# Two rearrangements in a hybrid-trunk kernel: the order of the matmuls inside a weight piece, and the addresses of its SBUF tiles

## The chip, the cores and the metric

The kernel runs on one core of one Trainium2 chip. The metric is the device time of one execution in microseconds. The kernel before takes 2270.38 us as the median of 3 runs (2270.03 to 2270.39).

## The reference, cut to what matters

Two layers act on 256 tokens of width 2048. Each has a token mixer (banded attention in the first layer, a gated linear recurrence in the second), a cross attention into 256 memory tokens, an output projection and a SwiGLU feed-forward part. Nearly all arithmetic is in the projections, each of the form "256 x K activations times K x N weights", in float32:

```python
mem_kv = rms_norm(mem, norm_mem[i]) @ w_mem_kv[i]
q_a, k_a, v_a, q_m = _split(h @ w_in_a[j], A_SPLITS)          # even layer
q_b, f_b, i_b, g_b, q_m = _split(h @ w_in_b[j], B_SPLITS)     # odd layer
x = x + jnp.concatenate([mix, mem_out], axis=-1) @ w_o[i]
gate, up = _split(rms_norm(x, norm_ffn[i]) @ w_gate_up[i], (D_FF, D_FF))
x = x + (jax.nn.silu(gate) * up) @ w_down[i]
```

with D_MODEL = 2048 and D_FF = 5632.

## The kernel before, in words

**Pieces.** All weights stream from HBM in pieces of 256 rows x 512 columns (512 KB), 768 pieces in all. SyncE issues one DMA for a piece into one of the four slots of `raw` (`piece`, L327). ScalarE copies it to `w_hi` in the type float32r (L488), VectorE writes `w_lo = raw - w_hi` (L833), and TensorE multiplies. The activations are kept in the same way as a pair of transposed tiles: `memT` (normed memory), `hT` (normed tokens), `mixT` (mixer output) and `gT` (feed-forward activations), each with a `_hi` and a `_lo` part. The product is the sum of three float32r products, hi x hi, lo x hi and hi x lo.

**Matmuls of a piece.** A piece has two blocks of 128 rows (`j`), and the tokens are two tiles of 128 (`tile`). So a piece is 2 x 3 x 2 = 12 matmuls, written by the generator `products` (L1362). The stationary operand is a 128 x 128 slice of the activations, the moving operand 512 columns of `w_hi` or `w_lo`. The result for tile 0 and the result for tile 1 accumulate in two neighbouring PSUM banks, `unit_bank0` and `unit_bank1`, or `unit_bank2` and `unit_bank3`. A "unit" is all the pieces that accumulate into one such pair: 8 pieces for K = 2048, 22 for K = 5632. The order inside a piece is written out by three nested loops.

**What orders the engines.** Every engine has its own program, and semaphores join them. `lo_ready` counts the pieces whose `w_lo` is written: TensorE waits for it ahead of a piece's first matmul, and SyncE waits for the count of four pieces back before it refills a slot of `raw`. `piece_used` is raised by the last matmul of a piece, and both ScalarE (L488) and VectorE (L833) wait for the count of four pieces back before they overwrite a slot of `w_hi` and `w_lo`. Between two pieces TensorE also runs the smaller work (transposes at L1385, attention at L1414 to L1463, recurrence at L1505 to L1549), at places that are fixed by lists of numbers.

**Where tiles lie.** The kernel gives every SBUF tile its address itself. `keep` hands out addresses one after another from the lowest free byte, 16512 per partition, rounded up to a multiple of `line`. Behind the kept tiles begins the arena, in which the tiles of the single stages share space. In the kernel before, twelve small tables (`ident` to `sum_two`) come first, `x_tok` is rounded up to a multiple of 2048, and since `x_tok`, `hT`, `raw`, `w_hi`, `w_lo`, `kmT_b`, `vm_b` have sizes that are multiples of 2048, all of these begin on a multiple of 2048. The arena begins on a multiple of 128.

Of the kernel before, what the change touches and what calls it, by code (L numbers as in the profile page):

```python
# [32 lines left out]
F32 = mybir.dt.float32  # L33
F32R = mybir.dt.float32r
I32 = mybir.dt.int32
# [4 lines left out]
P = 128  # L40
TILES = 2
SEQ = TILES * P
D = 2048
KT = D // P
COLS = 512
BLOCKS = D // COLS
# [4 lines left out]
HD_A, KV_A, GROUP_A = 64, 3, 8  # L51
HD_B, HEADS_B = 128, 12
GROUPS = 3
TOKEN_WIDTH = 1536
ROT = 8
# [89 lines left out]
def trunk(nc, x, mem, positions, norm_mix, norm_ffn, norm_mem, w_in_a, q_norm_a, k_norm_a, sinks_a,  # L145
          w_in_b, lb_logits, g_norm_b, w_mem_kv, q_norm_m, k_norm_m, w_o, w_gate_up, w_down, out):
    ctx = ExitStack()
    with ctx:

        place = [nc.sbuf_base]  # L150

        def at(name, shape, dtype, offset):
            t = nc.alloc_sbuf_tensor_at(name, [P] + shape, dtype, offset=offset)
            return t

        def keep(name, shape, dtype=F32, line=32):
            size = int(np.prod(shape)) * 4
            place[0] = -(-place[0] // line) * line
            t = at(name, shape, dtype, place[0])
            place[0] += size  # L160
            return t

        ident = keep("ident", [P])
        q_gain = keep("q_gain", [HD_A])
        k_gain = keep("k_gain", [HD_A])
        g_gain = keep("g_gain", [HD_B])
        cos = keep("cos", [TILES, ROT])
        sin = keep("sin", [TILES, ROT])
        ang = keep("ang", [TILES, ROT])
        turn = keep("turn", [TILES, ROT])  # L170
        freq = keep("freq", [ROT])
        pos_int = keep("pos_int", [TILES], I32)
        sum_sq = keep("sum_sq", [TILES, BLOCKS])
        sum_two = keep("sum_two", [TILES, 2])
        x_tok = keep("x_tok", [TILES, D], line=2048)
        hT = (keep("hT_hi", [KT, SEQ], F32R), keep("hT_lo", [KT, SEQ], F32R))
        raw = keep("raw", [RING, 2, COLS])
        w_hi = keep("w_hi", [RING, 2, COLS], F32R)
        w_lo = keep("w_lo", [RING, 2, COLS], F32R)
# [2 lines left out]
        tanh_ff = keep("tanh_ff", [TILES, COLS])  # L182
        act_ff = keep("act_ff", [TILES, COLS])
        squares = keep("squares", [COLS])
        level_mask = keep("level_mask", [LEVELS, P // 2])
        columns = keep("columns", [ROWS])
        sink = keep("sink", [KV_A * GROUP_A])
        minus_sink = keep("minus_sink", [KV_A * GROUP_A])
        lb_work = keep("lb_work", [4, HEADS_B])
        decay_table = keep("decay_table", [3, HEADS_B])  # L190
        decay_now = keep("decay_now", [3, 4])
        mem_sum_sq = keep("mem_sum_sq", [TILES, BLOCKS])
        mean_sq = keep("mean_sq", [TILES])
        rs = keep("rs", [TILES])
# [13 lines left out]
        inv = keep("inv", [TILES, GROUP_A])  # L208


        arena = -(-place[0] // 128) * 128
        assert arena + 2 * FT * SEQ * 4 <= nc.sbuf_usable_end, (arena, nc.sbuf_usable_end)
        gT = (at("gT_hi", [FT, SEQ], F32R, arena), at("gT_lo", [FT, SEQ], F32R, arena + FT * SEQ * 4))

        def arena_map(begin, end):
            here = [arena + begin]

            def take(name, shape, dtype=F32):
                t = at(name, shape, dtype, here[0])
                here[0] += -(-int(np.prod(shape)) * 4 // 32) * 32  # L220
                assert here[0] <= arena + end, name
                return t
            return take

        half = KT * SEQ * 4
        take = arena_map(0, 2 * FT * SEQ * 4)
# [7 lines left out]
        kmT, vm = (kmT_a, kmT_b), (vm_a, vm_b)  # L234
        take = arena_map(0, 2 * half)
        mixT = (take("mixT_hi", [KT, SEQ], F32R), take("mixT_lo", [KT, SEQ], F32R))
        take = arena_map(2 * half, 5 * half)
        q_a = take("q_a", [TILES, COLS])
        sq_a = take("sq_a", [TILES, COLS])
        qm_a = take("qm_a", [TILES, COLS])  # L240
# [12 lines left out]
        take = arena_map(2 * half, 2 * FT * SEQ * 4)  # L253
# [14 lines left out]
        take = arena_map(2 * half + 7 * TILES * COLS * 4, 2 * FT * SEQ * 4)  # L268
# [9 lines left out]
        unit_bank = [ctx.enter_context(nc.psum_tensor(f"unit_bank{n}", [P, COLS], F32)) for n in range(4)]  # L278
# [1065 lines left out]
        def _(pe):  # L1344
# [3 lines left out]
            def products(*units):  # L1348

                i = 0  # L1350
                for stationary, pair, kts, opens, closes, cols in units:
                    for n, kt in enumerate(kts):
                        yield i
                        if opens and n == 0 and t.any(f"unit_free{pair}"):
                            pe.wait_ge(sems[f"unit_free{pair}"], t.value(f"unit_free{pair}"))
                        s = slot[0] % RING
                        slot[0] += 1
                        pe.wait_ge(sems["lo_ready"], t.next("lo_ready"))
                        for j in range(2):
                            for m, (part, b) in enumerate(((0, w_hi), (1, w_hi), (0, w_lo))):  # L1360
                                for tile in range(TILES):
                                    ins = pe.matmul(unit_bank[2 * pair + tile][:, 0:cols],  # L1362
                                                    stationary[part][:, kt + j, tile * P:(tile + 1) * P],
                                                    b[:, s, j, 0:cols],
                                                    start=opens and n == 0 and j == 0 and m == 0,
                                                    stop=closes and n == len(kts) - 1 and j == 1 and m == 2)
                        ins.then_inc(sems["piece_used"], 1)
                        i += 1
                    if closes:
                        t.move(f"unit_free{pair}", TILES)  # L1370
# [224 lines left out]
            for i in products(unit(memT[0], 0)):  # L1595
                if i in (0, 2, 4, 6):
                    settled(0, 1)
                if i in (1, 2, 4):
                    c = (1, 2, 4).index(i) + 1
                    pe.wait_ge(sems[f"mem_in{c}"], t.next(f"mem_in{c}", 16))  # L1600
                    mem_block(c)
                if i == 6:
                    pe.wait_ge(sems["rows_in"], t.next("rows_in", 5 * 16))
                    pe.wait_ge(sems["free3"], t.value("free3"))
                    t.move("free3")
                    n = ROWS - NORM_MIX
                    pe.transpose(mix_bank[3][:, 0:n], rows[0:n, :], ident[0:n, 0:n]).then_inc(sems["full3"], 1)
            for i in products(unit(memT[0], 1)):
                if i % 2 == 0:
                    mem_block(i // 2)  # L1610
                if i == 7:
                    turn_keys()
            settled(0, 1)
            for i in products(unit(memT[1], 0)):
                if i % 2 == 0:
                    pe.wait_ge(sems[f"x_in{i // 2}"], t.next(f"x_in{i // 2}", 16))
                    x_block(i // 2)
# [126 lines left out]
```

## Time and profile before

| | |
|---|---|
| median of 3 runs | 2270.38 us |
| the profiled execution, its own time | 2270.38 us |
| its span in the profile | 2268.6 us |
| TensorE busy with matmuls | 2248.3 us, 99% |
| VectorE busy | 1270.5 us, 56% |
| ScalarE busy | 1006.7 us, 44% |
| DMA, mean over the span | 181 GB/s; the weight queue 59.1% of 16 engines |

The span is the stretch from the first to the last recorded instruction; the execution's own time has 1.8 us more around it. PE is TensorE's matmuls, PEld its loads of the stationary operand (which run beside matmuls), DVE is VectorE, ACT ScalarE, POOL GpSimd, SP SyncE. Matmuls are pipelined: the record of a 512-column matmul is 0.39 us long, and the next one starts 0.23 us after it. So a busy time says little of TensorE, and the distance between starts says much.

### The profile page before, as it was taken

The page shows a single profiled execution, that of the slowest core. Times are in us where ns is not written, and L with a number is a line of the kernel's source. Part 1 is how long each engine was busy: PE and PEld are TensorE (multiplying, and loading weights), DVE is VectorE, ACT ScalarE, POOL GpSimd, SP SyncE. Part 2 cuts the span into 40 slices and gives each one's busy share as a digit, 9 for nine tenths or more (in the row PEclk, how much of TensorE's full clock was granted, in tenths as well). Part 3 has the DMA queues.
Part 4 walks back from the last instruction along what each step waited for, and adds up shares of the span by engine and source line. Part 5 has one row for each costly group of instructions (what it writes and reads, how often), then busy time and mean ns, then how long its engine had stood idle before and what let it go on. Part 6 is the DMA issues. An engine that isn't in the chain of part 4 may idle for free.

```text
span 2268.6 us, 29587 instructions
## 1 busy us (share of the span) xinstructions
PE 2248.3 (99%) x10710; PEld 1878.3 (83%) x10710; DVE 1270.5 (56%) x1498; ACT 1006.7 (44%) x1242; POOL 55.9 (2%) x85
## 2 busy tenths in 40 slices
PE   8999999999999999999999999999999999999999
PEld 6888888888888888888888888888888888888887
DVE  6766665555555554555556666665555555554443
ACT  5656544444444444444443434354444444443332
POOL 2101000000000000000000000000000000000000
PEclk9999999999999999999999999999999999999999
DMA  7564446666666665565554545456666666666664
GB/s 246 176 202 125 133 162 196 187 192 188 191 186 185 194 186 193 194 191 190 177 146 144 166 148 167 138 189 185 193 188 191 186 192 186 191 187 205 203 198 137
DMA packets 213277, 410.29 MB, mean 181 GB/s; under 512 B 13264, under 2 KB 13516, under 8 KB 213196
## 3 DMA queue, kind: packets, MB, share of 16 engines
q1 hardware_dynamic: 212108, 407.11, 59.1%
q10 hardware_dynamic: 1088, 2.10, 0.2%
q8 instruction: 52, 0.85, 0.1%
q14 instruction: 29, 0.24, 0.0%
HBM read 407.06 MB, written 2.10 MB: 180 GB/s over the span
## 4 chain that ended last, share of the span: by engine, by line
PE 91%; DVE 1%; issue 1%; ACT 0%; POOL 0%; DVEq 0%
PE unit_bank L1362 85%; PE mix_bank L1385 2%; PE mix_bank L1520 2%; DVE w_lo L833 0%; PE mix_bank L1451 0%; PE mix_bank L1414 0%; PE mix_bank L1423 0%; PE mix_bank L1505 0%; ACT p_a L559 0%; DVE tanh_q L1065 0%; POOL head_rs L434 0%; PE mix_bank L1435 0%; PE mix_bank L1549 0%; PE mix_bank L1547 0%; PE mix_bank L1540 0%
## 5 line engine op out<-in xcount | busy, mean ns | idle before, releaser
L833 DVE TENSOR_TENSOR w_lo<-raw,w_hi 128x1024 fp32r<-128x1024 f32 x768 | 936.5, 1225 | 808.5 <-ACT w_hi L488 781.2
L488 ACT ACTIVATE w_hi<-raw 128x1024 fp32r<-128x1024 f32 x768 | 809.9, 1060 | 954.4 <-PE unit_bank L1362 930.6
L1362 PE MATMUL unit_bank<-w_hi,hT_hi 128*128 128x512 f32 (+1 forms) x1984 | 616.9, 392 | 0.0
L1362 PE MATMUL unit_bank<-w_hi,hT_lo 128*128 128x512 f32 (+1 forms) x1984 | 609.7, 388 | 0.0
L1362 PE MATMUL unit_bank<-w_lo,hT_hi 128*128 128x512 f32 (+1 forms) x1984 | 609.3, 388 | 0.0
L1362 PEld LDWEIGHTS unit_bank<-w_hi,hT_lo 128*128 128x128 f32 x1984 | 372.2, 188 | 76.9
L1362 PEld LDWEIGHTS unit_bank<-w_lo,hT_hi 128*128 128x128 f32 x1984 | 372.2, 188 | 76.8
L1362 PEld LDWEIGHTS unit_bank<-w_hi,hT_hi 128*128 128x128 f32 x1984 | 366.9, 188 | 70.8 <-issue 0.3
L1362 PE MATMUL unit_bank<-w_hi,gT_hi 128*128 128x512 f32 x704 | 217.1, 390 | 0.0
L1362 PE MATMUL unit_bank<-w_lo,gT_hi 128*128 128x512 f32 x704 | 216.8, 389 | 0.0
L1362 PE MATMUL unit_bank<-w_hi,gT_lo 128*128 128x512 f32 x704 | 216.8, 389 | 0.0
L1362 PEld LDWEIGHTS unit_bank<-w_lo,gT_hi 128*128 128x128 f32 x704 | 132.2, 188 | 27.6
L1362 PEld LDWEIGHTS unit_bank<-w_hi,gT_lo 128*128 128x128 f32 x704 | 132.2, 188 | 27.4
L1362 PEld LDWEIGHTS unit_bank<-w_hi,gT_hi 128*128 128x128 f32 x704 | 131.8, 188 | 27.0
L1362 PE MATMUL unit_bank<-w_hi,mixT_hi 128*128 128x512 f32 x256 | 80.8, 397 | 0.0
L1362 PE MATMUL unit_bank<-w_hi,mixT_lo 128*128 128x512 f32 x256 | 79.0, 390 | 0.0
L1362 PE MATMUL unit_bank<-w_lo,mixT_hi 128*128 128x512 f32 x256 | 78.9, 389 | 0.0
L1362 PEld LDWEIGHTS unit_bank<-w_lo,mixT_hi 128*128 128x128 f32 x256 | 48.1, 188 | 10.2
L1362 PEld LDWEIGHTS unit_bank<-w_hi,mixT_lo 128*128 128x128 f32 x256 | 48.1, 188 | 10.2
L1362 PEld LDWEIGHTS unit_bank<-w_hi,mixT_hi 128*128 128x128 f32 x256 | 46.5, 188 | 8.7 <-issue 0.2
L1362 PE MATMUL unit_bank<-w_hi,memT_hi 128*128 128x512 f32 x128 | 41.7, 408 | 4.9 <-DVE w_lo L833 4.9
L720 ACT ACTIVATE tanh_ff<-unit_bank,half_rs 128x512 f32<-128x512 f32 x44 | 27.9, 685 | 38.2 <-PE unit_bank L1362 38.2
(227 smaller groups left out, 1113.5 us busy)
## 6 DMA issues: line engine op xcount, KB each, us to landing
raw<-in_w_gate_up SPq DMA_DIRECT2D x352, 512.0 KB, 4.3
raw<-in_w_down SPq DMA_DIRECT2D x176, 512.0 KB, 4.5
raw<-in_w_in_b SPq DMA_DIRECT2D x104, 512.0 KB, 4.3
raw<-in_w_o SPq DMA_DIRECT2D x64, 512.0 KB, 4.1
raw<-in_w_in_a SPq DMA_DIRECT2D x40, 512.0 KB, 3.7
raw<-in_w_mem_kv SPq DMA_DIRECT2D x32, 512.0 KB, 4.0
mem_tok<-in_mem SPq DMA_DIRECT2D x4, 512.0 KB, 9.0
x_tok<-in_x SPq DMA_DIRECT2D x4, 512.0 KB, 7.7
```

What stands on the lines that cost most here:

```text
L488: act.activation(w_hi[:, s, :, :], raw[:, s, :, :], ACT.Copy).then_inc(sems["hi_ready"], 1)
L720: act.activation(tanh_ff[:, s, :], unit_bank[2 * pair + s][:, :], ACT.Tanh, scale=half_rs[:, s:s + 1]).then_inc(sems["tanh_ff_ready"], 1)
L833: dve.tensor_tensor(w_lo[:, s, :, :], raw[:, s, :, :], w_hi[:, s, :, :].bitcast(F32), ALU.subtract).then_inc(sems["lo_ready"], 1)
L1362: ins = pe.matmul(unit_bank[2 * pair + tile][:, 0:cols], stationary[part][:, kt + j, tile * P:(tile + 1) * P], b[:, s, j, 0:cols], start=o ...
L1385: ins = pe.transpose(mix_bank[b][:, n * P:(n + 1) * P], src[:, n * width:(n + 1) * width], ident[:, :])
L1520: ins = pe.matmul(mix_bank[b][:, h * P // 2:(h + 1) * P // 2], key[:, h, s * P:(s + 1) * P], late, start=True, stop=True)
```

## The change

It has two parts. The order of the instructions on ScalarE, VectorE, GpSimd and SyncE is the same before and after.

**A. The order inside a piece.** Before, for each block of rows, the three products are the outer loop and the token tiles the inner one. After, the token tiles are the outer loop, and the products come in the order hi x hi, (activation) hi x (weight) lo, lo x hi:

```diff
-                            for m, (part, b) in enumerate(((0, w_hi), (1, w_hi), (0, w_lo))):
-                                for tile in range(TILES):
-                                    ins = pe.matmul(unit_bank[2 * pair + tile][:, 0:cols],
-                                                    stationary[part][:, kt + j, tile * P:(tile + 1) * P],
-                                                    b[:, s, j, 0:cols],
+                            for tile in range(TILES):
+                                x_hi, x_lo = (m[:, kt + j, tile * P:(tile + 1) * P] for m in stationary)
+                                products = ((x_hi, w_hi), (x_hi, w_lo), (x_lo, w_hi))
+                                for m, (a, b) in enumerate(products):
+                                    ins = pe.matmul(unit_bank[2 * pair + tile][:, 0:cols], a, b[:, s, j, 0:cols],
                                                     start=opens and n == 0 and j == 0 and m == 0,
                                                     stop=closes and n == len(kts) - 1 and j == 1 and m == 2)
```

TensorE, the two row blocks of one piece in the last projection of a layer (K = 5632). A row names the bank written, then the moving and the stationary operand; numbers behind a name are those of the buffer. Before:

```order
L1362 MATMUL unit_bank2<-w_hi_65,gT_hi_96 128x512
L1362 MATMUL unit_bank3<-w_hi_65,gT_hi_96 128x512
L1362 MATMUL unit_bank2<-w_hi_65,gT_lo_97 128x512
L1362 MATMUL unit_bank3<-w_hi_65,gT_lo_97 128x512
L1362 MATMUL unit_bank2<-w_lo_66,gT_hi_96 128x512
L1362 MATMUL unit_bank3<-w_lo_66,gT_hi_96 128x512
```

The same place after:

```order
L1364 MATMUL unit_bank2<-w_hi_53,gT_hi_96 128x512
L1364 MATMUL unit_bank2<-w_lo_54,gT_hi_96 128x512
L1364 MATMUL unit_bank2<-w_hi_53,gT_lo_97 128x512
L1364 MATMUL unit_bank3<-w_hi_53,gT_hi_96 128x512
L1364 MATMUL unit_bank3<-w_lo_54,gT_hi_96 128x512
L1364 MATMUL unit_bank3<-w_hi_53,gT_lo_97 128x512
```

Before, every matmul writes another bank than the one ahead of it. After, three in a row write one bank, and the first two of the three have the same stationary slice. The compiled program has 6542 loads of the stationary operand and 6542 matmuls in both kernels, so the second of the two loads its slice again.

TensorE, the first matmuls behind the eight transposes of `act_ff` in the feed-forward loop, before:

```order
L1385 MATMUL mix_bank1<-ident_49,act_ff_70 128x128 x4
L1358 REGISTER_ALU
L1362 MATMUL unit_bank2<-w_hi_65,hT_hi_62 128x512
L1362 MATMUL unit_bank3<-w_hi_65,hT_hi_62 128x512
L1362 MATMUL unit_bank2<-w_hi_65,hT_lo_63 128x512
```

After:

```order
L1385 MATMUL mix_bank1<-ident_60,act_ff_58 128x128 x4
L1358 REGISTER_ALU
L1364 MATMUL unit_bank2<-w_hi_53,hT_hi_50 128x512
L1364 MATMUL unit_bank2<-w_lo_54,hT_hi_50 128x512
L1364 MATMUL unit_bank2<-w_hi_53,hT_lo_51 128x512
```

The small work stays at its place between two pieces; the wait for the piece is in both kernels ahead of its first matmul, and its last matmul is the twelfth in both.

**B. The addresses.** The small tables move behind the large tiles, `x_tok` begins at the lowest free byte, and the arena is rounded to 32 bytes where it was rounded to 128. The core of the diff:

```diff
-        def keep(name, shape, dtype=F32, line=32):
+        def keep(name, shape, dtype=F32):
             size = int(np.prod(shape)) * 4
-            place[0] = -(-place[0] // line) * line
+            place[0] = -(-place[0] // 32) * 32
...
-        ident = keep("ident", [P])
-        q_gain = keep("q_gain", [HD_A])
...
-        x_tok = keep("x_tok", [TILES, D], line=2048)
+        x_tok = keep("x_tok", [TILES, D])
...
-        arena = -(-place[0] // 128) * 128
+        arena = -(-place[0] // 32) * 32
```

| tile | byte address before | after |
|---|---|---|
| `x_tok` | 18432 (a multiple of 2048) | 16512 (128 past one) |
| `raw` | 67584 (a multiple of 2048) | 65664 (128 past one) |
| `w_hi` | 83968 (a multiple of 2048) | 82048 (128 past one) |
| `kmT_b` | 116736 (a multiple of 2048) | 114816 (128 past one) |
| arena, so `gT_hi`, `mixT_hi`, `memT0_hi` | 139008 (a multiple of 128; 1792 past one of 2048) | 138976 (32 past a multiple of 64; 1760 past one of 2048) |

`mem_tok`, `kmT_a`, `vm_a` and the tiles of the mixers lie in the arena at multiples of 128 from its beginning, so they move with it. The third edit in the diff, `5 * half` for `2 * half + 3 * half`, is the same number.

## Rows read from the trace of the kernel before

**Rows 1.** The page, busy time by engine, and the clock by slice
```profile
PE 2248.3 (99%) x10710; PEld 1878.3 (83%) x10710; DVE 1270.5 (56%) x1498; ACT 1006.7 (44%) x1242; POOL 55.9 (2%) x85
PEclk9999999999999999999999999999999999999999
```

**Rows 2.** The chain that ended last, two of its pieces in order: start us, us, what
```profile
490.73 43.54 PE unit_bank L1362 x192
...
535.14 43.54 PE unit_bank L1362 x192
```

**Rows 3.** Groups by line: busy us, mean ns, idle before and its releaser
```profile
L833 DVE TENSOR_TENSOR w_lo<-raw,w_hi 128x1024 fp32r<-128x1024 f32 x768 | 936.5, 1225 | 808.5 <-ACT w_hi L488 781.2
L488 ACT ACTIVATE w_hi<-raw 128x1024 fp32r<-128x1024 f32 x768 | 809.9, 1060 | 954.4 <-PE unit_bank L1362 930.6
```

**Rows 4.** Timeline around 1000 us: start us, us, what, [idle before and releaser]
```profile
999.99 0.61 PE L1362 MATMUL unit_bank<-w_hi,gT_hi 128*128 128x512 f32 x2
...
1000.25 1.06 ACT L488 ACTIVATE w_hi<-raw 128x1024 fp32r<-128x1024 f32 x1 [1.66 <-PE unit_bank L1362]
1000.45 0.62 PE L1362 MATMUL unit_bank<-w_hi,gT_lo 128*128 128x512 f32 x2
...
1000.90 0.62 PE L1362 MATMUL unit_bank<-w_lo,gT_hi 128*128 128x512 f32 x2
...
1001.34 1.23 DVE L833 TENSOR_TENSOR w_lo<-raw,w_hi 128x1024 fp32r<-128x1024 f32 x1 [1.49 <-ACT w_hi L488]
```

**Rows 5.** DMA issues: KB each, median us from issue to landing
```profile
raw<-in_w_down SPq DMA_DIRECT2D x176, 512.0 KB, 4.5
...
mem_tok<-in_mem SPq DMA_DIRECT2D x4, 512.0 KB, 9.0
```

**Rows 6.** TensorE's timeline: one group of L1414, and the end of one recurrence
```profile
177.59 1.89 PE L1414 MATMUL mix_bank<-kmT_a,qT_a 128*128 128x256 f32 x8
...
1239.27 1.05 PE L1540 MATMUL mix_bank<-v_b,wT 128*128 128x128 f32 x8
1240.16 0.39 PE L1547 MATMUL mix_bank<-v_b,wT_cross 128*128 128x128 f32 x2
1240.38 0.39 PE L1549 MATMUL mix_bank<-v_b,wT 128*128 128x128 f32 x2
1240.61 0.39 PE L1547 MATMUL mix_bank<-v_b,wT_cross 128*128 128x128 f32 x2
```

**Rows 7.** TensorE's timeline in the feed-forward loop
```profile
445.28 1.03 PE L1385 MATMUL mix_bank<-ident,act_ff 128*128 128x128 f32 x8
446.07 0.71 PE L1362 MATMUL unit_bank<-w_hi,hT_hi 128*128 128x512 f32 x2
446.62 0.62 PE L1362 MATMUL unit_bank<-w_hi,hT_lo 128*128 128x512 f32 x2
```

**Rows 8.** Single lines: duration ns minimum/median/maximum
```profile
L1362 PEld LDWEIGHTS unit_bank<-w_hi,hT_hi x1984: 186/188/192, 114.5 to 2022.3; 128*128 128x128 f32 x199
...
L1362 PEld LDWEIGHTS unit_bank<-w_hi,gT_hi x704: 187/188/192, 842.0 to 2262.6; 128*128 128x128 f32 x176
...
L1414 PE MATMUL mix_bank<-kmT_a,qT_a x16: 377/379/382, 169.5 to 179.1; 128*128 128x256 f32 x16
...
L1414 PE MATMUL mix_bank<-kmT_b,qT_b x16: 377/379/382, 1122.4 to 1132.0; 128*128 128x256 f32 x16
...
L866 DVE TENSOR_TENSOR hT_lo<-act_ff,hT_hi x32: 682/689/694, 68.7 to 1543.5; 128x512 fp32r<-128x512 f32 x32
...
L866 DVE TENSOR_TENSOR memT_lo<-act_ff,memT_hi x16: 683/692/725, 10.2 to 62.7; 128x512 fp32r<-128x512 f32 x16
```

**Rows 9.** Stretches: us, busy us by engine, clock, DMA share, GB/s
```profile
0.00:20.00 20.00, 9.44 (x37) 7.73 (x38) 9.39 (x12) 7.71 (x10) 0.74 (x7) 1.00 0.89 303
20.00:2260.00 2240.00, 2234.78 (x10658) 1867.46 (x10657) 1259.83 (x1485) 999.03 (x1233) 55.12 (x78) 1.00 0.59 180
```

**Rows 10.** Timeline of the start
```profile
8.56 1.06 ACT L488 ACTIVATE w_hi<-raw 128x1024 fp32r<-128x1024 f32 x1 [6.48 <-DMA raw<-in_w_mem_kv]
...
12.74 1.19 PE L1362 MATMUL unit_bank<-w_hi,memT_hi 128*128 128x512 f32 x2 [4.95 <-DVE w_lo L833]
```

More of the change, by code:

```diff
@@ L161, in keep @@
             return t
-        ident = keep("ident", [P])
-        q_gain = keep("q_gain", [HD_A])
[L165 to L174, printed above, removed]
-        x_tok = keep("x_tok", [TILES, D], line=2048)
+        x_tok = keep("x_tok", [TILES, D])
         hT = (keep("hT_hi", [KT, SEQ], F32R), keep("hT_lo", [KT, SEQ], F32R))
@@ L184, in trunk @@
         squares = keep("squares", [COLS])
+        ident = keep("ident", [P])
         level_mask = keep("level_mask", [LEVELS, P // 2])
         columns = keep("columns", [ROWS])
+        q_gain = keep("q_gain", [HD_A])
+        k_gain = keep("k_gain", [HD_A])
+        g_gain = keep("g_gain", [HD_B])
         sink = keep("sink", [KV_A * GROUP_A])
         minus_sink = keep("minus_sink", [KV_A * GROUP_A])
+        pos_int = keep("pos_int", [TILES], I32)
+        cos = keep("cos", [TILES, ROT])
+        sin = keep("sin", [TILES, ROT])
+        ang = keep("ang", [TILES, ROT])
+        turn = keep("turn", [TILES, ROT])
+        freq = keep("freq", [ROT])
         lb_work = keep("lb_work", [4, HEADS_B])
@@ L191, in trunk @@
         decay_now = keep("decay_now", [3, 4])
+        sum_sq = keep("sum_sq", [TILES, BLOCKS])
+        sum_two = keep("sum_two", [TILES, 2])
         mem_sum_sq = keep("mem_sum_sq", [TILES, BLOCKS])
@@ L236, in trunk @@
         mixT = (take("mixT_hi", [KT, SEQ], F32R), take("mixT_lo", [KT, SEQ], F32R))
-        take = arena_map(2 * half, 5 * half)
+        take = arena_map(2 * half, 2 * half + 3 * half)
         q_a = take("q_a", [TILES, COLS])
```

## The prediction, made before the changed kernel ran

> **What bounds the kernel now.** I read the page's busy times first: matmuls on TensorE are busy for 99% of the span, VectorE 56%, ScalarE 44%, and the clock is at its upper level in all 40 slices [rows 1]. Next comes the chain of waits. It is a string of pieces "PE unit_bank L1362", most of them 192 matmuls long, one behind the other [rows 2]. 43.54 us for 192 matmuls is 226.8 ns from start to start. There are 768 weight pieces [rows 3] of 12 matmuls, 9216 in all, and 9216 x 226.8 ns = 2090 us (the few narrower ones taken as full). So 92% of the span of 2268.6 us is one number, the distance between two starts of a 512-column matmul. The rest is the start, the small matmuls and the tail.
>
> Then I looked at whether anything feeds that stream late. The grouped lines show the opposite: ScalarE's idle time ahead of L488 (930.6 us) is ended by TensorE, and VectorE's ahead of L833 by ScalarE [rows 3]. Both wait until TensorE lets go of a slot. The timeline shows one piece [rows 4]: a slot of w_hi comes free and ScalarE starts at 1000.25; VectorE ends at 1001.34 + 1.23 = 1002.57. TensorE has three more pieces in front of this one, and a piece is 12 x 0.2268 = 2.72 us, so it comes to it near 999.99 + 3 x 2.72 = 1008.15. The split is ready 5.6 us early. The DMA of the next piece for that slot is issued at 1002.57 and ScalarE wants it 4 x 2.72 us after 1000.25, at 1011.13; that leaves 8.6 us, and a landing takes 4.5 [rows 5].
>
> **Part A, the order of the matmuls.** Nothing is added or removed: 12 matmuls and 12 loads a piece, the same wait ahead of the first, the same release behind the last. What can change is only the 226.8 ns, by three things that a pair of neighbours has: whether they share the moving operand, the bank, or the stationary slice.
>
> The moving operand: before, matmuls 1 to 4 of six read w_hi and 5 and 6 read w_lo. The pairs start at 999.99, 1000.45, 1000.90 [rows 4], so the step is the same 0.45 us for two where the moving operand stays and where it changes. Cost 0.
>
> The bank: in the 512-column stream the bank changes at every matmul, so the row that would tell is missing there, and I go by the nearest ones. L1540 writes eight products with no accumulation, and the next group starts 1240.16 - 1239.27 = 0.89 us later: 111 ns each. L1547 and L1549 follow in pairs, the second adding onto the very columns that the first has just written, and a pair takes 1240.38 - 1240.16 = 0.22 us, again 111 ns each [rows 6]. So adding onto the same bank at once costs nothing at a distance half as long as the one here. From below: L1414 has eight 256-column float32 matmuls in 1.89 us, the last of which has a record of 0.38 us [rows 8], so they are (1.89 - 0.38) / 7 = 216 ns apart, 11 ns less than 226.8. If all of this 11 ns were the price of a change of bank, it would go for 8 of 12 matmuls, 6144 in all: -68 us. But among those eight the bank changes too (L1414 writes two to a bank), and the average stays at 216. From above: transposes stand 1.03 us for eight [rows 7], (1.03 - 0.27) / 7 = 109 ns by a record of 0.27 us, 2 to 3.4 ns less than the accumulating pairs; were 3.4 ns the price of staying in a bank, 6144 x 3.4 = +21 us. A full drain (0.39 us record less 0.23) would be +0.16 us each, and the 111 ns pairs exclude it. I take 0, the row that it is nearest to.
>
> The stationary slice: it is loaded again, so a load stays in front of every matmul. A load is recorded with 188 ns [rows 8], but 128-column products follow each other every 111 ns, each with a load of its own [rows 6], so the load path has 116 ns in hand under 226.8. If a load of the slice already there cost nothing, that path would only get idler. The bound on the good side is the same 11 ns for the 4 of 12 matmuls that repeat a slice, 3072 x 11 = -34 us; on the bad side, the first matmul behind transposes shows the dearest stall of this kind: 0.71 us for two where others have 0.62, 0.09 us [rows 7]. That stall belongs to a change of the kind of matmul, is paid at the same places after, and I take 0.
>
> Here stands a rule that speaks for another outcome. The distance is 226.8 ns at the upper clock [rows 1, 2]. The Trainium skill, page "TensorE: Matmul & The Clock Gate", section "Back-to-back issue gap", gives N / 2.4 + 2.5 ns, which is 215.8 ns for 512 columns. The trace has 11 ns more and does not agree; the page's figure is not for float32r. If the 11 ns were waste that this order removes, the rule would become true after the change; that is the first rival.
>
> **Part B, the addresses.** Compute operands first. `kmT_a` lies 1792 bytes past a multiple of 2048, so its first 1024-byte slice crosses such a boundary, and `kmT_b` begins on one; as moving operands both give 379 ns [rows 8]. The stationary loads out of `gT` (1792 past) and `hT` (on it) are both 188 ns, and VectorE's writes to `memT_lo` (1792 past) and `hT_lo` (on it) have medians of 692 and 689 ns [rows 8]. So leaving the 2048 grid costs nothing that I can see. An operand that starts 32 bytes past a multiple of 64, as gT, mixT and memT do after, is not in the trace at this size. Below: 0. Above: a load could become twice as slow in its steady pace, 111 to 222 ns, and would still fit under 226.8. Work of VectorE and ScalarE on arena tiles has the 5.6 us in hand; the short serial stretches of the mixers do not, but one more beat on them is nanoseconds. I take 0.
>
> DMA: the landings in raw now begin 128 bytes past a multiple of 2048, and mem_tok's at 32 past one of 64. For the stream, a landing would have to grow from 4.5 to 8.6 us before TensorE noticed. Only the start has no such cover: in the first 20 us DMA is at 0.89 and 303 GB/s, against 0.59 later [rows 9]; ScalarE waits 6.48 us for its first piece, and TensorE's first real matmul waits for VectorE until 12.74 us [rows 10]. Below: 0. Above: the four memory blocks, 2.1 MB, take 6.9 us at 303 GB/s; at double time that is +6.9 us at most. I take 0, as all landings of the trace are on the grid and none shows what leaving it costs. By the Trainium skill, page "DMA: Bandwidth & Descriptors", section "How a descriptor splits into AXI transactions", a 2 KB run off a 256-byte boundary takes 9 transactions for 8; the sum would be some 0.5 us longer, an estimate for the start alone, and no run here shows it.
>
> **Sum.** 2270.4 (the profiled execution's own time, which is also the median) + 0 (A) + 0 (B) = 2270.4 us.
>
> **Rivals.**
> 1. The 11 ns goes where a matmul repeats the bank or the slice: 2270.4 - 34 = 2236 us for the slice, 2202 for the bank. For it: the gap to 216 is there in the trace and unexplained. Against: it does not move with the moving operand, and L1414 changes banks without it.
> 2. Slower, at the start: landings off the grid. Place: the first 20 us, where TensorE waits for pieces; price up to +6.9, so 2271 to 2277 us. It decides as soon as a landing is longer than the DMA queue's cover, which the start does not have and the stream does (8.6 us).
> 3. Slower, everywhere: three accumulations in a row into one bank, or loads from the arena at 32 bytes past, lengthen the distance. At 3.4 ns for 6144 matmuls, 2291 us. Against: the 111 ns pairs.
>
> **How the numbers follow.** Two runs of this kernel can be told apart at about 0.2%, 4.5 us. No change: 0.70, all of it within 0.2%. Rival 1: 0.13. Rival 2: 0.09, of which about 0.04 stays within 0.2% and 0.05 does not. Rival 3: 0.08. So faster 0.13, same 0.74, slower 0.13. The range must hold 8 in 10: the first case and the second, 0.79, with a little of the third: 2267 to 2280 us. It leaves out the first rival, which would land far away.
>
> **What would show it.** The distance in the long pieces of the chain: 43.54 us for 192 matmuls if I am right; 42.1 if the 11 ns goes for two matmuls in three (the bank), 42.8 for one in three (the slice); above 43.6 for rival 3, and then in gT, mixT and memT alone if it is the arena, or everywhere if it is the bank. The first matmul at 12.74 us, and the landing of mem_tok at 9.0 us, tell of rival 2; the landing of raw at 4.5 us may move with no effect. Records of loads at 188 ns and of `w_lo` at 1225 ns should stay. I am wrong if the distance between 512-column matmuls depends on the bank or the slice of the neighbour, which this trace cannot show.

## The result, and the profile after

The kernel after takes 2292.79 us, the median of 4 runs (2292.48 to 2293.86), against 2270.39 (4 runs) before: 1.0099 times as long, with an interval of 1.0082 to 1.0116. The forecast was 2270.4 us, in a range from 2267 to 2280. The span of the profiled execution grew from 2268.6 to 2291.1 us, by 22.5.

The page of the kernel after, busy time by engine, shows that no other engine has more work [rows 1]:

```profile
PE 2272.7 (99%) x10710; PEld 1880.4 (82%) x10710; DVE 1271.0 (55%) x1498; ACT 1007.5 (44%) x1242; POOL 55.9 (2%) x85
```

The chain that ended last names the place. In the kernel before, a piece of the feed-forward loop has 192 matmuls out of `hT` in 43.54 us [rows 2], and a piece of the last projection has 264 out of `gT` (start us, us, what); then their like in the kernel after:

```profile
909.49 59.86 PE unit_bank L1362 x264
```

```profile
494.41 43.54 PE unit_bank L1364 x192
...
915.45 61.85 PE unit_bank L1364 x264
```

Out of `hT` the distance from start to start is still 43.54 / 192 = 226.8 ns (every second piece of that loop has 43.57 us, the last one 43.66). Out of `gT` it went from 59.86 / 264 = 226.7 to 61.85 / 264 = 234.3 ns. TensorE's timeline of the kernel after shows it step by step, at the place of [rows 4]:

```profile
999.81 0.40 PE L1364 MATMUL unit_bank<-w_hi,gT_hi 128*128 128x512 f32 x1
1000.04 0.39 PE L1364 MATMUL unit_bank<-w_lo,gT_hi 128*128 128x512 f32 x1
1000.28 0.39 PE L1364 MATMUL unit_bank<-w_hi,gT_lo 128*128 128x512 f32 x1
1000.51 0.40 PE L1364 MATMUL unit_bank<-w_hi,gT_hi 128*128 128x512 f32 x1
```

The steps are 0.23 to 0.24 us wherever they fall, behind a repeated slice, in a repeated bank and at a change of bank alike. TensorE is idle in none of them. From the starts of the first matmul out of each tile in both traces, the stages grew so:

| stationary tile | wide matmuls | growth, us |
|---|---|---|
| `memT` | 384 | 1.7 |
| `mixT` | 768 | 2.2 + 2.2 |
| `gT` | 2112 | 8.0 + 8.0 |
| `hT` (all four stages) | 5856 | 0.7 |

That is 22.1 us where the tiles of the arena are read and 0.7 in the four other stages together; the first wide matmul starts 0.4 us earlier, which leaves the 22.4 us by which the last one is later. Shared out over the matmuls, the growth is 7.6 ns out of `gT`, 5.7 out of `mixT` and 4.4 out of `memT`. In an unbroken run of 72 out of `mixT` it is 7.4 (16.34 us before, 16.87 after); why the stages with small work in between lose less for each matmul, no run here shows. The record of a load is the same as before [rows 8], and that of a matmul is longer, first in the kernel before, then in the kernel after (ns minimum/median/maximum; the ends of matmul records are modelled, so the starts above are the firmer measure):

```profile
L1362 PE MATMUL unit_bank<-w_hi,gT_hi x704: 389/389/476, 842.3 to 2262.8; 128*128 128x512 f32 x176
```

```profile
L1364 PEld LDWEIGHTS unit_bank<-w_hi,gT_hi x704: 187/188/192, 845.9 to 2285.4; 128*128 128x128 f32 x176
L1364 PE MATMUL unit_bank<-w_hi,gT_hi x704: 392/397/481, 846.1 to 2285.6; 128*128 128x512 f32 x176
```

### The profile page after: what moved, and what is told of

The parts are those of the page before. It is cut to its first block, busy times and chain, and to the rows that moved or that the text cites. A ratio compares the mean times of both kernels' runs of the same rounds, so it can differ in the third digit from the quotient of the medians.

```text
span 2291.1 us, 29587 instructions
## 1 busy us (share of the span) xinstructions
PE 2272.7 (99%) x10710; PEld 1880.4 (82%) x10710; DVE 1271.0 (55%) x1498; ACT 1007.5 (44%) x1242; POOL 55.9 (2%) x85
## 4 chain that ended last, share of the span: by engine, by line
PE 92%; DVE 1%; issue 0%; ACT 0%; POOL 0%; DVEq 0%; ACTq 0%
PE unit_bank L1364 86%; PE mix_bank L1385 2%; PE mix_bank L1520 2%; PE mix_bank L1451 0%; PE mix_bank L1414 0%; DVE w_lo L833 0%; PE mix_bank L1423 0%; PE mix_bank L1505 0%; DVE tanh_q L1065 0%; PE mix_bank L1460 0%; PE mix_bank L1435 0%; PE mix_bank L1549 0%; PE mix_bank L1547 0%; PE mix_bank L1540 0%; PE mix_bank L1530 0%
## 5 line engine op out<-in xcount | busy, mean ns | idle before, releaser
L1364 PE MATMUL unit_bank<-w_hi,hT_hi 128*128 128x512 f32 (+1 forms) x1984 | 778.0, 392 | 0.0
L1364 PE MATMUL unit_bank<-w_hi,hT_lo 128*128 128x512 f32 (+1 forms) x1984 | 771.2, 389 | 0.0
L1364 PE MATMUL unit_bank<-w_lo,hT_hi 128*128 128x512 f32 (+1 forms) x1984 | 770.2, 388 | 0.0
L1364 PE MATMUL unit_bank<-w_hi,gT_hi 128*128 128x512 f32 x704 | 279.5, 397 | 0.0
L1364 PE MATMUL unit_bank<-w_hi,gT_lo 128*128 128x512 f32 x704 | 279.1, 396 | 0.0
L1364 PE MATMUL unit_bank<-w_lo,gT_hi 128*128 128x512 f32 x704 | 279.0, 396 | 0.0
L1364 PE MATMUL unit_bank<-w_hi,mixT_hi 128*128 128x512 f32 x256 | 103.3, 403 | 0.0
L1364 PE MATMUL unit_bank<-w_hi,mixT_lo 128*128 128x512 f32 x256 | 101.4, 396 | 0.0
L1364 PE MATMUL unit_bank<-w_lo,mixT_hi 128*128 128x512 f32 x256 | 101.4, 396 | 0.0
L1364 PE MATMUL unit_bank<-w_lo,memT_hi 128*128 128x512 f32 x128 | 51.5, 402 | 0.0
```

The costliest lines, as they stand in the source:

```text
L1364: ins = pe.matmul(unit_bank[2 * pair + tile][:, 0:cols], a, b[:, s, j, 0:cols], start=opens and n == 0 and j == 0 and m == 0, stop=closes ...
```

## The experiments

**Which part of the change, and which address.** Three kernels. The first is the kernel after with the arena where it was:

```diff
-        arena = -(-place[0] // 32) * 32
+        arena = -(-place[0] // 128) * 128
```

> The kernel after with one edit: the arena is rounded to 128 bytes again (139008). The new order of the matmuls and the 128-past-2048 addresses of x_tok, raw, w_hi, w_lo stay. Theory 1 (a stationary slice that starts 32 bytes past a multiple of 64 costs TensorE some 7 ns a matmul; 3264 of the 9216 wide matmuls take theirs from the arena): all of the loss goes, 2270.4 us, and the 264-matmul pieces of the last projection go from 61.85 back to 59.86 us. Theory 2 (the new order costs, for instance three accumulations in a row into one bank, but only in units with gT, mixT, memT): 2292 us stays. Theory 3 (leaving the 2048 grid costs): 2292 us stays.

Measured: 2289.08 us (5 runs) against 2270.58, ratio 1.0082 (1.0068 to 1.0095). Less than 4 of the 22 us came back. Theory 1, my own, fell with it: the arena is at the very address of before and still slow. Its chain:

```profile
914.11 61.34 PE unit_bank L1364 x264
```

61.34 / 264 = 232.3 ns, neither 226.7 nor 234.3.

The second is the kernel before with part A of the change alone.

> The kernel before with part A alone: the token tile is the outer loop, the three products the inner one; every address as before. Theory 1 (stationary address): 2270.4 us, 264 matmuls in 59.86 us. Theory 2 (order): 2292 us.

Measured: 2270.66 us (11 runs), ratio 1.0000 (0.9991 to 1.0009). Its chain:

```profile
910.00 59.86 PE unit_bank L1364 x264
```

The order of the matmuls costs nothing. The third is the kernel before with the arena shifted by 96 bytes:

```diff
-        arena = -(-place[0] // 128) * 128
+        arena = -(-place[0] // 128) * 128 + 96
```

> The kernel before with one edit: 96 bytes are added to the arena's beginning, so gT, mixT, memT begin 96 past a multiple of 128 (32 past one of 64), as in the kernel after. Order and all other addresses as before. Theory 1: 2293 us, the whole loss, and 264 matmuls in 61.9 us. Theory 2 (order, or order and address together): 2270.4 us. Theory 3 (2048 grid of the kept tiles): 2270.4 us.

Measured: 2293.19 us (4 runs), ratio 1.0099 (1.0084 to 1.0115), the whole loss from one edit of an address, with the old order:

```profile
450.87 43.54 PE unit_bank L1362 x192
...
916.21 61.85 PE unit_bank L1362 x264
```

So the arena's address can make the loss alone, yet putting it back in the kernel after does not cure it. Each of the three theories is contradicted by one kernel: the arena's own address by the first, the order by the second, the kept tiles off the 2048 grid by the third, in which they are on it. Beside the order, which costs nothing, what the first kernel still has of the change is that the kept tiles, w_hi and w_lo among them, begin 128 bytes past a multiple of 2048. Either these addresses cost by themselves, or what counts is where the two operands lie to each other.

**Streams of matmuls by themselves.** The kernel of the probe loads x, writes two float32r tiles, `st` and `mv`, both on a multiple of 2048, and runs lines like this one, which differ in the offsets (in elements of 4 bytes), the bank and the columns:

```python
for i in range(24): pe.matmul(bank[i % 2][0:128, 0:512], st[:, 8 + 128 * (i % 4):136 + 128 * (i % 4)], mv[:, 0:512], ...)
```

> Not the computation of the reference: it copies x to the output, and TensorE runs streams of 24 float32r matmuls (128 x 128 stationary, 512 columns), one source line for each kind, on random data. The lines differ in where the stationary slice begins (0, 32, 64, 96, 16, 48, 4, 128 bytes past a multiple of 2048), where the moving operand begins (32, 64, 16, 128 bytes), both at 32, one bank throughout against two in turn, three in a row in one bank, 256 columns, a stationary of 64 columns, and one slice loaded again and again. Theory 1: distance 227 ns at stationary offsets 0, 64 and 128, about 234 at 32 and 96, more or equal at 16, 48 and 4; moving offsets and banks change nothing. Theory 2: 227 for every offset with two banks in turn, 234 where a bank is repeated. If the load and the moving operand share a read path, 32 on both sides costs more than on one, and 256 columns lose the same nanoseconds per matmul as 512.

The steps are read from the starts of two neighbouring lines, divided by the number of matmuls. TensorE's timeline of that kernel, a part of the first, and the lines on bank and slice:

```profile
27.42 5.61 PE L46 MATMUL bank<-mv,st 128*128 128x512 f32 x24
32.87 5.75 PE L47 MATMUL bank<-mv,st 128*128 128x512 f32 x24
...
94.28 5.62 PE L58 MATMUL bank<-mv,st 128*128 128x512 f32 x24
99.74 5.63 PE L59 MATMUL bank<-mv,st 128*128 128x512 f32 x24
105.22 5.76 PE L60 MATMUL bank<-mv,st 128*128 128x512 f32 x24
110.81 5.76 PE L61 MATMUL bank<-mv,st 128*128 128x512 f32 x24
116.41 3.02 PE L62 MATMUL bank<-mv,st 128*128 128x256 f32 x24
...
133.18 5.62 PE L66 MATMUL bank<-mv,st 128*128 128x512 f32 x24
138.64 5.76 PE L67 MATMUL bank<-mv,st 128*128 128x512 f32 x24
144.24 5.61 PE L68 MATMUL bank<-mv,st 128*128 128x512 f32 x24
```

L46 has both operands at 0: 5.45 / 24 = 227 ns. L47 has the slice 32 bytes further: 5.59 / 24 = 233 ns. L58 has both 32 bytes further: 5.46 / 24 = 227.5 ns. That one line decides between the two readings: an address of its own costs nothing, the distance between the operands does. The lines on the other offsets, not shown, refute my expectation for 64 and 128 bytes, which cost as much as 32 (233 ns), and for moving offsets, which cost as well: 233 ns with the moving operand 32 ahead and 232.5 at 128, but only 229 at 64. Offsets of 4, 16 and 48 bytes cost 232 to 234. L59 writes one bank all the time (228 ns), L60 the same at distance 32 (233), L61 three in a row into a bank at distance 32 (233), L66 loads one slice again and again (227.5) and L67 the same at distance 32: bank and slice add 1.3 ns at most in the streams, and nothing in the second kernel above. Two lines with a stationary operand of 64 columns, not shown, have 230 ns at distance 0 and 232 at 32: the cost shrinks from 6 ns to 2. At 256 columns there is none (119 ns at 0, 118 at 32).

**Whether the kernel obeys the distance.** Theory 4 from here on: what counts is the address of the stationary slice minus that of the moving operand, modulo 256 bytes. The `_lo` tiles lie a multiple of 256 bytes behind their `_hi` tiles, so one number holds for all products of a stage. For the matmuls out of the arena it is 0 in the kernel before (139008 - 83968), 96 for the kernel after and for the third kernel above, 128 for the first. Two kernels test it. In the first, the kernel after has its arena 128 past a multiple of 256, as its w_hi has:

```diff
-        arena = -(-place[0] // 32) * 32
+        arena = -(-(place[0] - 128) // 256) * 256 + 128
```

> The kernel after with one edit: the arena begins at 139136, 128 past a multiple of 256, as w_hi and w_lo do (82048, 98432). Everything is still off the multiples of 256 and 2048, and the new order stays. Theory 4 (what counts is the distance between the addresses of the stationary slice and the moving operand, modulo 256: 0 gives 227 ns, 128 gives 232 to 233, 96 gives 234): 2270.4 us, 264 matmuls in 59.86 us. Rival 5 (an arena operand must itself lie on a multiple of 256, or the kept tiles on a multiple of 2048): 2289 us or more stays.

Measured: 2271.56 us (11 runs), ratio 1.0004 (0.9995 to 1.0013). The loss is gone with x_tok, hT, raw, w_hi, w_lo and the arena all 128 past a multiple of 256, and with the new order:

```profile
446.55 43.54 PE unit_bank L1364 x192
...
909.88 59.86 PE unit_bank L1364 x264
```

In the second, the kernel before gets w_hi and w_lo shifted, and the arena with them:

```diff
+        place[0] += 128
         w_hi = keep("w_hi", [RING, 2, COLS], F32R)
```

> The kernel before with one edit: 128 bytes are left free ahead of w_hi, so w_hi and w_lo begin 128 past a multiple of 256 and the arena follows to 139136, also 128 past; hT stays on a multiple of 256. Order as before. Theory 4: the picture is turned round. gT, mixT and memT have the distance 0 and keep 227 ns (264 matmuls in 59.86 us), the 5952 matmuls out of hT lose 6 ns each (192 matmuls in 44.6 to 44.7 us for 43.54), together +36 us, 2306 us. Rival 5 (each operand's own address): hT is untouched and stays at 43.54, the arena off its grid loses, 2289 us.

Measured: 2302.74 us (4 runs) against 2270.57, ratio 1.0142 (1.0127 to 1.0158), and the picture is turned round, as said (the added line makes L1363 of L1362):

```profile
450.73 44.62 PE unit_bank L1363 x192
...
984.62 59.86 PE unit_bank L1363 x264
```

`hT` has never moved here, and it is the one that is slow: (44.62 - 43.54) / 192 = 5.6 ns, and 5856 x 5.6 = 33 us for the 32.2 measured and the 36 expected. Rival 5 is refuted by both.

**How the cost depends on the distance.**

> Not the computation of the reference: it copies x to the output, and TensorE runs streams of 48 float32r matmuls on random data, one source line for each distance from the stationary slice to the moving operand: 0, 32, 64, ... 480 bytes; then both operands at 96, both at 128, the moving one at 256 and at 192, and 384 and 256 columns at distances 0 and 32. Theory 4: 227 ns at 0 and 256 and for both pairs at equal offsets, 232 to 235 at the others, a period of 256 bytes, and 192 (moving 64 ahead cost only 229 in the first sweep) between. If the period were 512, 256 would be slow; the trace of before (arena at distance 1792, 256 modulo 512, at 227 ns) speaks against it. With 256 columns the distance should cost nothing, by the first sweep (119 ns for 0, 118 for 32).

TensorE's timeline; from L46 to L54 the slice is 0, 32, 64, ... 256 bytes ahead, in L62 both operands are at 96, in L63 both at 128, in L64 the moving operand is at 256 and in L65 at 192:

```profile
26.99 11.05 PE L46 MATMUL bank<-mv,st 128*128 128x512 f32 x48
37.88 11.35 PE L47 MATMUL bank<-mv,st 128*128 128x512 f32 x48
49.07 11.36 PE L48 MATMUL bank<-mv,st 128*128 128x512 f32 x48
60.27 11.40 PE L49 MATMUL bank<-mv,st 128*128 128x512 f32 x48
71.51 11.32 PE L50 MATMUL bank<-mv,st 128*128 128x512 f32 x48
82.67 11.37 PE L51 MATMUL bank<-mv,st 128*128 128x512 f32 x48
93.87 11.16 PE L52 MATMUL bank<-mv,st 128*128 128x512 f32 x48
104.86 11.36 PE L53 MATMUL bank<-mv,st 128*128 128x512 f32 x48
116.06 11.05 PE L54 MATMUL bank<-mv,st 128*128 128x512 f32 x48
126.94 11.35 PE L55 MATMUL bank<-mv,st 128*128 128x512 f32 x48
...
205.12 11.10 PE L62 MATMUL bank<-mv,st 128*128 128x512 f32 x48
216.06 11.07 PE L63 MATMUL bank<-mv,st 128*128 128x512 f32 x48
226.97 11.05 PE L64 MATMUL bank<-mv,st 128*128 128x512 f32 x48
237.86 11.36 PE L65 MATMUL bank<-mv,st 128*128 128x512 f32 x48
```

| distance, bytes | 0 | 32 | 64 | 96 | 128 | 160 | 192 | 224 | 256 |
|---|---|---|---|---|---|---|---|---|---|
| ns from start to start | 227 | 233 | 233 | 234 | 232.5 | 233 | 229 | 233 | 227 |

The period is 256 bytes: L55 to L61 (288 to 480 bytes, most not shown) repeat the values of 32 to 224 within 0.3 ns, and L62 to L65 fit. For the kernels: 96 bytes cost 7.4 ns, times 3264 matmuls 24 us, for 22.4 and 22.6 measured (after, and the arena at +96; the missing part is in mixT and memT, as above); 128 bytes cost 5.8 ns, 19 us for 18.5 measured. The table says further that 192 is cheap, which no rule of "aligned or not" would. So one more kernel: the one before with `+ 192` at the arena.

> The kernel before with one edit: 192 bytes are added to the arena's beginning (139200), so its stationary slices lie 192 bytes past w_hi and w_lo modulo 256. Theory 4 with the sizes of the second sweep: 192 costs 229.2 - 226.8 = 2.4 ns, so 3264 x 2.4 = +8 us, 2278 us, and 264 matmuls in 60.5 us; a third of the loss that 96 bytes brought, though the shift is twice as large. Rival 6 (any start off a multiple of 128 or 256 costs the arena's operands the same): 2289 to 2293 us.

Measured: 2277.21 us (8 runs) against 2270.50, ratio 1.0028 (1.0018 to 1.0039), 6.7 us for the 8 expected; rival 6 is refuted. Its chain:

```profile
911.70 60.44 PE unit_bank L1362 x264
```

60.44 / 264 = 228.9 ns, as in the table.

**Which pair, how many columns, which type.**

> Not the computation of the reference: it copies x to the output, and TensorE runs streams of 48 matmuls on random data, one source line for each kind. First: which pair counts. Stationary and moving operand both alternate between 0 and 32 bytes, once in step (each matmul has distance 0 to its own slice, but the slice loaded during its stream, that of the next one, is 32 off), once in counter-step. If a matmul is slowed by the load that runs beside it, the stream in step takes 233 ns and the one in counter-step 227; if its own slice counts, the other way round. With one of the two alternating, half of the matmuls are at 32: 230 ns either way. Slices 256 bytes apart: 227; 288 bytes apart: some 232, since three of four are off. Then 416, 448, 480 and 496 columns at distances 0 and 32: 384 showed no cost and 512 has 6.5 ns, so it should appear somewhere between. Then bfloat16, 512 columns (1024 bytes), at distances 0, 32, 128 and moving 32 ahead, and float32 with 256 columns at 0 and 32: no cost if it takes a long 4-byte stream to show it.

TensorE's timeline. L55 both at 0, L56 alternating in step, L57 in counter-step, L58 the slice alone alternating, L59 the moving operand alone; L68 and L69 are 496 columns at 0 and 32; L70 and L71 bfloat16 at 0 and 32; L74 and L75 float32 at 0 and 32, where a matmul is recorded in two halves, so 48 are 96, and the record of the whole line is compared, since L76 behind it is of another type:

```profile
31.41 11.04 PE L55 MATMUL bank<-mv,st 128*128 128x512 f32 x48
42.30 11.30 PE L56 MATMUL bank<-mv,st 128*128 128x512 f32 x48
53.44 11.20 PE L57 MATMUL bank<-mv,st 128*128 128x512 f32 x48
64.47 11.42 PE L58 MATMUL bank<-mv,st 128*128 128x512 f32 x48
75.73 11.21 PE L59 MATMUL bank<-mv,st 128*128 128x512 f32 x48
86.78 11.05 PE L60 MATMUL bank<-mv,st 128*128 128x512 f32 x48
...
167.18 10.88 PE L68 MATMUL bank<-mv,st 128*128 128x496 f32 x48
177.90 11.04 PE L69 MATMUL bank<-mv,st 128*128 128x496 f32 x48
188.78 10.54 PE L70 MATMUL bank<-mb,sb 128*128 128x512 bf16 x48
199.15 10.52 PE L71 MATMUL bank<-mb,sb 128*128 128x512 bf16 x48
209.51 10.52 PE L72 MATMUL bank<-mb,sb 128*128 128x512 bf16 x48
...
230.23 20.88 PE L74 MATMUL bank<-mf,sf 128*128 128x256 f32 x96
250.95 20.88 PE L75 MATMUL bank<-mf,sf 128*128 128x256 f32 x96
```

In step 11.14 / 48 = 232 ns, in counter-step 11.03 / 48 = 230 ns. I had expected one of them at 227 and got neither, so this does not tell whether a matmul suffers from its own slice or from the one that is loaded beside it. bfloat16 takes 216 ns at every distance tried, and a float32 half 216 ns at both. The kernel after agrees for float32: at L1414 `kmT_b` begins 128 past a multiple of 256 and its stationary `qT_b` 224 past one, distance 96, and its group of eight halves, at 1134.20 us, takes the 1.89 us that L1414 has in [rows 6]. Both types keep the pace although their loads differ, 98 ns in bfloat16 and 190 in float32, for 188 in float32r. Where only one operand alternates I had expected 230 ns twice: it is 235 for the slice (L58) and 230 for the moving operand (L59). Slices 256 bytes apart have 227 ns, as expected (L60), and slices 288 apart, where three of four are off, 231 for some 232 expected (L61, not shown). At 496 columns of float32r the distance of 32 costs 10.88 / 48 against 10.72 / 48, 3.3 ns. From the starts of lines not shown, at 480 columns it costs nothing (217 ns both), at 448 and 416 2 and 3 ns, and at 384 nothing (173 ns both, in the second sweep): it is no steady function of the columns.

## Why the prediction was wrong

**The bound.** Right. TensorE's distance from start to start sets 92% of the span, and the whole change of time is a change of that number. The other engines' covers held, no wait was added.

**Part A, 0 us.** Right, and shown: the order alone gives a ratio of 1.0000 (0.9991 to 1.0009). The new order at distance 0 with the new addresses costs nothing either (1.0004), and with the arena at +96 the old order loses what the kernel after loses (2293.19 and 2292.79 us). The three arguments were right in their result. The one on the bank rested on float32 rows, and I misread them: "eight matmuls" at L1414 were four in two halves each, the "eight products" of L1540 were four, and each pair of L1547 or L1549 was one matmul, so 111 ns is the distance between halves and not between matmuls. The streams in one bank now show it for float32r.

**Part B, compute operands, 0 us.** This step failed. It said: "So leaving the 2048 grid costs nothing that I can see", from `kmT_a` against `kmT_b`, and for loads and writes from tiles at 1792 bytes past against tiles on the grid. There are three faults. 1792 is a multiple of 256, so those rows compare distance 0 with distance 0; the sample held no other case. The matmuls out of `kmT` are float32, and float32 has no such cost at 32 bytes (L75 of the last streams) nor at 96 (L1414 in the kernel after), so they could not have told even off the 256 grid. And I asked how long a load may become before it shows (116 ns in hand), as if a load and a stream could only meet by one waiting for the other's end. The records show loads at 188 ns in both kernels, while the distance between matmuls grew from 226.7 to 234.3 ns: the stream itself became slower, by 7.6 ns, at a distance of 96 bytes between its two operands. That is the term I had put at 0. For the unseen case the honest end of the range was the per-matmul row of rival 3, and I had given it 0.08 and left it outside.

**Part B, DMA, 0 us.** Right in result: `mem_tok` lands in 8.8 us after and 9.0 before [rows 5], and the first real matmul starts at 12.30 after and 12.74 before [rows 10]. Neither the 6.9 us of rival 2 nor the half microsecond estimated for runs off a 256-byte boundary is to be seen.

**Rival 1.** Refuted: repeating a bank or a slice gains nothing in the streams (228 and 227.5 ns).

**Rival 3.** Its time, 2291 us, is right by luck: the 3.4 ns for 6144 matmuls by the bank stand for 7 ns for 3264 matmuls by the address. Its other cause, loads from the arena at 32 bytes past, named the right tiles, but what counts is their distance to w_hi and w_lo and not their own address. The sign that I had named for it is the one seen: the long pieces of gT, mixT and memT alone.

The 11 ns between 226.8 and 216 stay unexplained: bfloat16 and float32 halves run at 216 with loads between, float32r at 227 at its best distance. The Trainium skill, page "TensorE: Matmul & The Clock Gate", section "Step-by-step: what each phase is for", says that PE has two independent SBUF read ports and that loading the next weights does not steal read bandwidth from the running matmul. The bfloat16 and float32 lines agree (216 ns at every distance tried); the float32r lines do not (227 to 234 by the distance of two addresses alone). A collision of the two reads in SBUF is my reading of that; no run here shows it directly.

## What to carry to other kernels

Two operands can each be well placed and badly placed to each other: where a stream of wide float32r matmuls sets the time, put the stationary and the moving tiles at the same address modulo 256 bytes, and look again after each new small tile in front of them. If the trace holds only one value of a quantity that a change moves, equal times across it are no evidence that the quantity is free; ask what the compared rows have in common before using them, here modulo 256 and the data type. No version faster than the kernel before turned up; distance 0 is the lowest of the eight measured.

## What the runs showed of the hardware that was not expected

- float32r, 128 x 128 stationary, 512 columns at the upper clock: 227 ns from start to start at distance 0 modulo 256 bytes, 229 at 192, 232.5 to 234 at 32, 64, 96, 128, 160 and 224, and 232 to 234 at 4, 16 and 48.
- The absolute addresses do not matter: both operands at 32, 96 or 128 give 227 to 228 ns. A repeated bank or a repeated slice changes it by 1.3 ns at most.
- bfloat16, 512 columns: 216 ns at distances 0, 32 and 128 and with the moving operand 32 ahead; a half of a float32 matmul of 256 columns: 216 ns at 0 and 32, and no growth at 96.
- Open: whose slice counts, the matmul's own or the next one's, why 256, 384 and 480 columns show nothing where 416, 448, 496 and 512 do, and why a stationary operand of 64 columns shows less.
